# HGRN part of a hybrid decoder step: gate group ahead of the value group and between the levels; first half of the decay differences ahead of the fourth masked sum; last values product at the end of the tile

## The chip, the cores and the metric

The kernel runs on one core of one Trainium2 chip. The metric is the device time of one execution in microseconds (us), the median of several runs. Engines by the names of the profile: PE is TensorE, DVE VectorE, ACT ScalarE, POOL GpSimd, SP SyncE (which only issues transfers here).

## What is computed

One step of a one-layer hybrid decoder on 2048 prompt tokens and 64 sample tokens, model width 1024. The input projection has eight groups of 512 columns: four for an attention part, four for an HGRN2 part (query, forget, value, gate). The change concerns the HGRN2 part, a gated linear recurrence with 4 heads of 128 x 128 state:

```
b    = cumsum(log f)                                # over the tokens of a chunk
att  = q . k * exp(b_t - b_s)  for s <= t           # per channel, then summed
o    = att @ v + (q * exp(b)) @ S
S'   = exp(b_last) * S + (k * exp(b_last - b))^T @ v
out  = rms_norm(o) * silu(gate)                     # then the output projection
```

## The kernel before

The program has four passes, each closed by a barrier of all engines: `pass_projections` (projections of the attention groups for 17 tiles of 128 tokens, then the HGRN2 part), `pass_attention`, `pass_samples`, `pass_output`. Only the HGRN2 part of `pass_projections` is touched; it is written for each engine by hand, and the engines meet through semaphores. Each engine takes its instructions in the order written.

The HGRN2 part works on one tile t of 128 tokens per `step(t, ...)`, t = 0 to 15; in the same step PE projects the four groups of the next tile i = t + 1 and DVE, ACT and POOL prepare that tile's operands. A product of two fp32 values is made as three products of split operands (lines 92 to 94), 24 matmuls of 512 columns for a group, 6 for a quarter (`product_quarter`).

- `group(i, p, g)` (PE): group g = 0 query, 1 forget, 2 value, 3 gate. Before the change groups 0 and 2 land in PSUM bank 0, groups 1 and 3 in bank 1. A group waits until ACT has copied out what stood in its bank.
- `levels(t, h)` (PE, lines 876 and 877): for head h the seven masked parts of the decay products, 14 matmul rows in the trace, into two banks that all heads share; so levels of head h wait until DVE has multiplied those of head h - 1 by the mask.
- `keep_pairs(t, h)` (DVE): the mask product (line 737) and the masked sum (line 741), which gives `att`.
- `out_rows(t, pt, h)` (PE, lines 885 and 886): the values product `att @ v` plus the state's part; it waits for `att`.
- `key_rows`, `head_columns`, `gains` (PE): transposes of keys, of query and forget columns, and the state's gain.
- `forget(i)` (DVE, lines 747 to 752), `decays(i)` (ACT, logarithm, line 585), `cumulate(i)` (DVE, running sum, line 759): the decay of the next tile.
- `differences` (DVE): for each half of two heads 16 subtractions and copies in `decay_differences` (lines 127 to 136), into the buffer `lv[hf]`; the second half, hf = 1, waits until `out_rows` of head 3 has read that buffer.
- `exps(i, hf)` (ACT, line 589): the exponential of a half in place.
- `operands(i)` (POOL, `decay_products`, lines 145 to 150): for each half 14 products with q and k, in place.
- `gate_input`, `inputs_q`, `inputs_f`, `value_input`, `q_columns` (ACT): copies of projections out of PSUM with their activation. A change of function costs an ACT_TABLE_LOAD.
- `o_stats` (ACT), `o_norm`, `carry` (DVE), `gated` (POOL), `store` (SP): norm of the output rows, the new state, the gating and the store.
- `again(t)` (SP): loads the split x of tile t into one of two buffers when tile t - 2 has been projected.

Before the change the order of a step on PE is: group 0; levels 0; first half of group 1; levels 1; values 0; second half of group 1; levels 2; keys; values 1; head columns; levels 3; values 2; first half of group 2; values 3; second half of group 2; first half of group 3; gains; second half of group 3. On DVE: masked sums 0, 1, 2; forget; masked sum 3; cumulate; both halves of the differences; norm; carry. On ACT: gate of tile t; query and forget of tile i; keys; query columns; logarithm; exponential 0; values; exponential 1; norm.

Of the kernel before, what the change touches and what calls it, by code (L numbers as in the profile page):

```python
# [8 lines left out]
ACT = mybir.ActivationFunctionType  # L9
# [7 lines left out]
P = 128  # L17
# [4 lines left out]
NP = SEQ // P  # L22
NT = NP + 1
# [44 lines left out]
PIECES = 4  # L68
# [3 lines left out]
def after(eng, sem, count):  # L72

    if not isinstance(count, int) or count > 0:
        eng.wait_ge(sem, count)
# [44 lines left out]
def decay_differences(dve, b, lv, blocks, last, n0=0):  # L120

    for slot, width in blocks:
        b_lo, b_up, ref = level_views(b, width)
        d_lo, d_up, _ = level_views(lv[:, slot - n0, :], width)
        dve.tensor_tensor(d_up, b_up, ref, ALU.subtract)
        dve.tensor_tensor(d_lo, ref, b_lo, ALU.subtract)
    pair = b.rearrange("p (n w) -> p n w", w=2)
    first = pair[:, :, 0:1].broadcast_to([P, pair.shape[1], 2])  # L130
    dve.tensor_tensor(lv[:, LEAF_Q - n0, :].rearrange("p (n w) -> p n w", w=2), pair, first, ALU.subtract)
    dve.tensor_tensor(lv[:, LEAF_K - n0, :].rearrange("p (n w) -> p n w", w=2), first, pair, ALU.subtract)
    dve.tensor_copy(lv[:, LEAF_QE - n0, :], b)
    run = b.rearrange("p (n w) -> p n w", w=last)
    end = run[:, :, last - 1:last].broadcast_to([P, run.shape[1], last])
    return dve.tensor_tensor(lv[:, LEAF_KD - n0, :].rearrange("p (n w) -> p n w", w=last), end, run, ALU.subtract)  # L136
# [14 lines left out]
                              k[:, None, :].broadcast_to([P, 2, n]), ALU.mult)  # L151


LAST = NT - 1

EVICT = list(range(NP - 1)) + [LAST, NP - 1]
# [2 lines left out]
def pass_projections(nc, io, keep):  # L159


    with ExitStack() as ctx:
# [7 lines left out]
        w_hi = [sb(f"w_hi{g}", [P, KD, GW], F32R) for g in range(4)]  # L170
# [62 lines left out]
        def half(ap, hf):  # L233
            return ap[:, hf * 2 * P:(hf + 1) * 2 * P]

        def col(t):
            return rstd[:, t:t + 1]

        @block.sync
        def _(sp):  # L240
# [21 lines left out]
            def again(t):  # L262

                if t == 0:
                    sp.wait_ge(s["proj"][3], NT - 1)
                elif t == 1:
                    sp.wait_ge(s["proj"][3], NT)
                else:
                    sp.wait_ge(s["proj"][7], t - 1)
                sp.wait_ge(s["x2_store"][t % 2], 32 * (t // 2 + 1))  # L270
                sp.dma_start(f32(x_hi[t % 2][:, :, :]).rearrange("p k t -> p (k t)"), io["xh_s"][t]).then_inc(s["x2_load"][t % 2], 16)
                sp.dma_start(f32(x_lo[t % 2][:, :, :]).rearrange("p k t -> p (k t)"), io["xl_s"][t]).then_inc(s["x2_load"][t % 2], 16)
# [181 lines left out]
        def _(act):  # L454
# [7 lines left out]
            def pieces(g):  # L462
                for n in range(g * PIECES, (g + 1) * PIECES):
                    piece(n)
# [94 lines left out]
            def gate_input(i, p):  # L559
                act.wait_ge(s["proj"][7], i + 1)  # L560
                after(act, s["o_out"], i - 1)
                act.activation(gate[:, p], bank[1], ACT.Silu, scale=col(i)).then_inc(s["gate"], 1)

            def inputs_q(i):
                act.wait_ge(s["proj"][4], i + 1)
                after(act, s["qT_ps"], i)
                act.activation(q_tok, bank[0], ACT.Silu, scale=col(i)).then_inc(s["q_tok"], 1)

            def inputs_f(i):
                act.wait_ge(s["proj"][5], i + 1)  # L570
                after(act, s["sT_ps"], i)
                act.activation(s_tok, bank[1], ACT.Sigmoid, scale=col(i)).then_inc(s["s_tok"], 1)

            def q_columns(i):
                act.wait_ge(s["qT_ps"], i + 1)
                after(act, s["operands"], 2 * i)
                act.activation(qT, tps.rearrange("p h t -> p (h t)"), ACT.Copy).then_inc(s["qT"], 1)

            def value_input(i, p):
                act.wait_ge(s["proj"][6], i + 1)  # L580
                act.activation(v_tok[:, p], bank[0], ACT.Copy, scale=col(i)).then_inc(s["v_tok"], 1)

            def decays(i):
                act.wait_ge(s["f_clamped"], i + 1)
                act.activation(lfT, lfT, ACT.Ln).then_inc(s["log_f"], 1)

            def exps(i, hf):
                act.wait_ge(s["diff"], 2 * i + hf + 1)
                act.activation(lv[hf], lv[hf], ACT.Exp).then_inc(s["decay"], 1)  # L589
# [10 lines left out]

            def step(t, pt, more):
                i, p = t + 1, 1 - pt
                gate_input(t, pt)
                inputs_q(i)
                inputs_f(i)
                act.wait_ge(s["kdT_ps"], t + 1)
                after(act, s["gain_ps"], t)
                act.activation(kd_tok, kps.rearrange("p h d -> p (h d)"), ACT.Copy).then_inc(s["kd_tok"], 1)
                q_columns(i)
                decays(i)  # L610
                if more:
                    exps(i, 0)
                value_input(i, p)
                if more:
                    exps(i, 1)
                    tile_decay(p)
                o_stats(t)

            act.wait_ge(s["x_lo"], NT)
            inputs_q(0)  # L620
            pieces(7)
            inputs_f(0)
            act.wait_ge(s["store_q"][0], 32 * 9)
            act.wait_ge(s["store_q"][1], 32 * 8)
            q_columns(0)
            decays(0)
            exps(0, 0)
            value_input(0, 0)
            exps(0, 1)
            tile_decay(0)  # L630
            act.wait_ge(s["store_v"], 16 * NT)
            act.wait_ge(s["store_g"], 16 * NT)
            for t in range(NP):
                step(t, t % 2, t < NP - 1)
            gate_input(NP, 0)

        @block.vector
        def _(dve):
# [6 lines left out]
            def pieces(g):  # L645
                for n in range(g * PIECES, (g + 1) * PIECES):
                    piece(n)
# [79 lines left out]
            norm_qk(NP - 1)  # L727
            pieces(5)
            pieces(6)
            pieces(7)  # L730

            def keep_pairs(t, h):

# [26 lines left out]
                last.then_inc(s["cumsum"], 1)  # L760
                dve.wait_ge(s["cumsum"], i + 1)

            def differences(i, t):
                for hf in range(2):
                    if t is not None:
                        dve.wait_ge(s["av"], 4 * t + 2 * hf + 2)
                        dve.wait_ge(s["kdT_ps"], t + 1)
                    decay_differences(dve, half(bT, hf), lv[hf], all_levels, P).then_inc(s["diff"], 1)

            def o_norm(t):  # L770
                o3 = o_out.rearrange("p (h v) -> p h v", h=H)
# [16 lines left out]
            for p in range(2):  # L788
                dve.wait_ge(s["store_q"][p], 32 * (9 - p))
            forget(0)  # L790
            cumulate(0)
            differences(0, None)

            def step(t, pt, more):
                i = t + 1
                keep_pairs(t, 0)
                keep_pairs(t, 1)
                keep_pairs(t, 2)
                forget(i)
                keep_pairs(t, 3)  # L800
                if more:
                    cumulate(i)
                    differences(i, t)
                o_norm(t)
                carry(t, pt)

# [5 lines left out]
        def _(pe):  # L812
# [26 lines left out]
                job(g, LAST)  # L839
                job(g, NP - 1)  # L840

            def group(i, p, g, halves=(0, 1)):

                if 0 in halves:
                    pe.wait_ge(s["x2_load"][p], 32 * (i // 2 + 1))
                    if i == 0 and g < 2:
                        pe.wait_ge(s["qk_norm"], 2 * NT - 2)
                    after(pe, s[("v_tok", "gate", "q_tok", "s_tok")[g]], i if g < 2 else i + 1)
                for b in range(PIECES):
                    if b // 2 in halves:  # L850
                        if i == 0:
                            pe.wait_ge(s["w_lo"], (4 + g) * PIECES + b + 1)
                        mm = product_quarter(pe, bank[g % 2], x_hi[p], x_lo[p], w_hi[g], w_lo[g], b)
                if 1 in halves:
                    mm.then_inc(s["proj"][4 + g], 1)

            def head_columns(i, t):
# [46 lines left out]
            def step(t, pt):  # L904
                i, p = t + 1, 1 - pt
                group(i, p, 0)
                levels(t, 0)
                group(i, p, 1, (0,))
                levels(t, 1)
                out_rows(t, pt, 0)  # L910
                group(i, p, 1, (1,))
                levels(t, 2)
                key_rows(t)
                out_rows(t, pt, 1)
                head_columns(i, t)
                levels(t, 3)
                out_rows(t, pt, 2)
                group(i, p, 2, (0,))
                out_rows(t, pt, 3)
                group(i, p, 2, (1,))  # L920
                group(i, p, 3, (0,))
                gains(t, pt)
                group(i, p, 3, (1,))

            group(0, 0, 0)
            group(0, 0, 1)
# [1048 lines left out]
```

## Time and profile before

| | |
|---|---|
| median of 3 runs | 1761.52 us (1758.78 to 1763.17) |
| the profiled execution | 1758.49 us, of which its span 1756.7 us |
| mean granted TensorE clock | 0.962 |
| busy share of the span | PE 90%, DVE 56%, ACT 43%, POOL 28% |
| the HGRN2 steps | about 441 to 992 us of the span |

All times in the rows below are counted from the start of the span. Busy shares are averages over four passes with different limits; the steps are read from windows inside them.

### The profile page before, as it was taken

Reading aid. Unit: us, or ns where it says so; the run is one execution under the profiler, and the core shown is the slowest. Engines: PE = TensorE matmul, PEld = TensorE weight load, DVE = VectorE, ACT = ScalarE, POOL = GpSimd, SP = SyncE. Lnnn points to the kernel's source line nnn. Section 1 sums busy time; section 2 is a strip of 40 time slices with the busy share of each in tenths; the row PEclk is TensorE's granted clock in tenths of the full one; section 3 lists DMA queues with packets and bytes.
Section 4 is the critical chain, followed back from the end, with each engine's and each line's share of the span. In section 5 each row is a group of like instructions: output and inputs, shape, how many; then the busy total and the mean of one; then the engine's idle time right before and its main releaser. Section 6 shows DMA issues by size and latency. Waiting matters only on the chain. (4 is left out here: it accounts for less than half of the span.)

```text
span 1756.7 us, 25192 instructions
## 1 busy us (share of the span) xinstructions
PE 1577.5 (90%) x9156; PEld 1277.6 (73%) x9156; DVE 982.8 (56%) x2316; ACT 753.1 (43%) x1074; POOL 485.7 (28%) x636
## 2 busy tenths in 40 slices
PE   6799999997999999999999689999999568299998
PEld 5688888886887788778887567767777445177776
DVE  4322222254677667766776489888888624523332
ACT  5333333345444544453445266666666422211110
POOL 1433223341544664466446200000000010121211
PEclk9999999998999999999999889999999869699999
DMA  8444433445010101010100331000000286534442
GB/s 298 179 144 144 144 144 144 179 141 170 26 37 31 55 31 37 30 55 31 37 31 31 116 121 66 30 25 13 14 24 13 82 279 222 162 117 138 150 142 72
DMA packets 79762, 171.48 MB, mean 98 GB/s; under 512 B 9122, under 2 KB 15906, under 8 KB 79650
## 3 DMA queue, kind: packets, MB, share of 16 engines
q1 hardware_dynamic: 79650, 170.00, 28.0%
q8 instruction: 69, 1.13, 0.3%
q14 instruction: 43, 0.35, 0.1%
HBM read 113.35 MB, written 56.62 MB: 97 GB/s over the span
## 5 line engine op out<-in xcount | busy, mean ns | idle before, releaser
L92 PE MATMUL h_banks<-h_w_hi,h_x_hi 128*128 128x512 f32 x1088 | 435.4, 400 | 23.0 <-DVE h_x_lo L651 16.5
L94 PE MATMUL h_banks<-h_w_hi,h_x_lo 128*128 128x512 f32 x1088 | 426.9, 392 | 0.0
L93 PE MATMUL h_banks<-h_w_lo,h_x_hi 128*128 128x512 f32 x1088 | 426.7, 392 | 0.0
L92 PEld LDWEIGHTS h_banks<-h_w_hi,h_x_hi 128*128 128x128 f32 x1088 | 206.6, 190 | 65.9 <-DVE h_x_lo L651 17.3
L94 PEld LDWEIGHTS h_banks<-h_w_hi,h_x_lo 128*128 128x128 f32 x1088 | 206.0, 189 | 44.3
L93 PEld LDWEIGHTS h_banks<-h_w_lo,h_x_hi 128*128 128x128 f32 x1088 | 206.5, 190 | 40.7
L145 POOL TENSOR_TENSOR h_stage_or_levels<-h_stage_or_levels,h_qk_or_hgrn 128x128 f32<-128x128 f32 x192 | 105.8, 551 | 283.2 <-ACT h_stage_or_levels L589 283.2
L1078 ACT ACTIVATE p_scores<-p_scores,p_nmx 128x256 f32<-128x256 f32 (+15 forms) x128 | 153.1, 1196 | 5.6 <-DVE p_nmx L1129 5.4
L1214 PE MATMUL p_ops<-p_V,p_WT 128*128 128x128 f32 x1088 | 146.4, 280 | 8.8 <-ACT p_WT L1087 8.4
L1214 PEld LDWEIGHTS p_ops<-p_V,p_WT 128*128 128x128 f32 x1088 | 132.6, 193 | 15.6 <-ACT p_WT L1087 14.2
L1124 DVE CUSTOM_DVE_ANT_0 p_scores<-p_sps,p_zero 128x512 f32<-128x512 f32 x192 | 122.2, 686 | 15.8 <-PE p_sps L1188 15.6
L737 DVE TENSOR_TENSOR h_qk_or_hgrn<-h_banks,h_mask 128x896 f32<-128x896 f32 x64 | 69.7, 1090 | 105.7 <-PE h_banks L877 105.7
L1087 ACT ACTIVATE p_WT<-p_tps 128x512 f32<-128x512 f32 (+3 forms) x160 | 84.6, 529 | 84.7 <-PE p_tps L1201 84.4
L589 ACT ACTIVATE h_stage_or_levels<-h_stage_or_levels 128x2560 f32<-128x2560 f32 x32 | 75.1, 2347 | 102.6 <-DVE h_stage_or_levels L136 102.6
L83 PE MATMUL y_yps<-w_out_hi,y_mT_hi 128*128 128x512 f32 x272 | 111.0, 408 | 7.8 <-DVE y_yt L1850 6.4
L741 DVE TENSOR_REDUCE h_qk_or_hgrn<-h_qk_or_hgrn 128x128 f32<-128x896 f32 x64 | 111.2, 1738 | 2.2
L876 PE MATMUL h_banks<-h_stage_or_levels 128*128 128x128 f32 x768 | 97.7, 277 | 14.6 <-POOL h_stage_or_levels L150 14.6
L876 PEld LDWEIGHTS h_banks<-h_stage_or_levels 128*128 128x128 f32 x768 | 93.1, 191 | 23.9 <-POOL h_stage_or_levels L150 21.4
L1403 POOL MEMSET s_Q<- 128x1024 f32 x1 | 1.0, 951 | 393.6 <-POOLq L58 393.6
L83 PE MATMUL y_yps<-w_out_lo,y_mT_hi 128*128 128x512 f32 x272 | 108.5, 399 | 0.0
L83 PE MATMUL y_yps<-w_out_hi,y_mT_lo 128*128 128x512 f32 x272 | 108.4, 399 | 0.0
L402 POOL TENSOR_TENSOR h_qk_or_hgrn<-h_qk_or_hgrn,h_qkg 128x1024 f32<-128x1024 f32 x17 | 42.7, 2513 | 202.4 <-DVE h_qk_or_hgrn L673 202.4
(218 smaller groups left out, 2642.4 us busy)
## 6 DMA issues: line engine op xcount, KB each, us to landing
h_stage_or_levels<-in_w_in SPq DMA_DIRECT2D x32, 512.0 KB, 6.3
h_xs_sq_or_tok<-in_xT SPq DMA_DIRECT2D x17, 512.0 KB, 5.9
h_qk_or_hgrn<-in_x SPq DMA_DIRECT2D x17, 512.0 KB, 6.1
tmp_xh_s<-h_x_hi SPq DMA_DIRECT2D x17, 512.0 KB, 3.2
tmp_xl_s<-h_x_lo SPq DMA_DIRECT2D x17, 512.0 KB, 4.4
h_x_hi<-tmp_xh_s SPq DMA_DIRECT2D x17, 512.0 KB, 3.6
h_x_lo<-tmp_xl_s SPq DMA_DIRECT2D x17, 512.0 KB, 4.5
s_kc<-in_cache_k SPq DMA_DIRECT2D x32, 256.0 KB, 3.7
```

Of the source, the lines that this page charges most:

```text
L83: mm = eng.matmul(out, a[:, k, :], b[:, k, cols], start=(k == 0 and a is x_hi and b is w_hi), stop=(k == KD - 1 and a is x_lo))
L92: eng.matmul(out, x_hi[:, k, :], w_hi[:, k, :], start=(k == 0), stop=False)
L93: eng.matmul(out, x_hi[:, k, :], w_lo[:, k, :], start=False, stop=False)
L94: mm = eng.matmul(out, x_lo[:, k, :], w_hi[:, k, :], start=False, stop=(k == KD - 1))
L145: pool.tensor_tensor(e_up, e_up, q_up, ALU.mult)
L589: act.activation(lv[hf], lv[hf], ACT.Exp).then_inc(s["decay"], 1)
L741: dve.tensor_reduce(att[:, h % 2], masked.rearrange("p l t -> p t l"), AX.X, ALU.add).then_inc(s["att"], 1)
L876: pe.matmul(lps[:, n, :], l[:, n, c], l[:, n, c], start=True, stop=True)
L1078: act.activation(row, row, ACT.Exp, bias=nmx[:, n % 2, m:m + 1], accum_out=ls[:, u % 2, m, h:h + 1]).then_inc(s["exp"], 1)
L1087: act.activation(WT[:, g % 2, 0:w // P, :], tps[g % 2][:, 0:w // P, :], ACT.Copy).then_inc(s["wT"], 1)
L1124: dve.tensor_tensor_reduce(sc[m][:, n % (4 - m), c0:c0 + w], sps[k % 4][:, 0:w], add, SCALE, -3e38, ALU.add, ALU.max, mx[:, n % 2, m, c:c ...
L1214: mm = pe.matmul(ops[u % 2][:, h, :], WT[:, g % 2, b, :], V[:, kb, h * DV:(h + 1) * DV], start=(kb == 0), stop=(kb == TILES[u]))
```

## The change

The projection of the gate moves ahead of that of the values, in quarters placed between the levels; group 1 is done whole, right behind group 0, ahead of levels 0. From tile 1 on the gate lands in bank 0 and the values in bank 1 (`bank_of`). Head columns come after values 0, three places earlier. Values 3 (`out_rows` of head 3) closes the step. On DVE `forget` stands ahead of masked sum 2, `cumulate` and the first half of the differences ahead of masked sum 3, the second half behind it. On ACT the gate of tile i is copied between the logarithm and exponential 0, no longer the gate of tile t at the start of the step. SP's `again` waits for both the value and the gate group. Ahead of the first step, ACT's copy of the forget group and DVE's `forget(0)` stand ahead of the last weight pieces, and the copies of values and gate ahead of the exponentials.

```diff
+def bank_of(i, g):
+    if i > 0 and g >= 2:
+        return 3 - g
+    return g % 2
...
+                    sp.wait_ge(s["proj"][6], t - 1)
                     sp.wait_ge(s["proj"][7], t - 1)
...
             def step(t, pt, more):                      # scalar
                 i, p = t + 1, 1 - pt
-                gate_input(t, pt)
                 inputs_q(i)
                 inputs_f(i)
+                q_columns(i)
                 act.wait_ge(s["kdT_ps"], t + 1)
                 after(act, s["gain_ps"], t)
                 act.activation(kd_tok, ...)
-                q_columns(i)
                 decays(i)
+                gate_input(i, p)
                 if more:
                     exps(i, 0)
                 value_input(i, p)
...
             inputs_q(0)
+            inputs_f(0)
             pieces(7)
-            inputs_f(0)
...
             decays(0)
+            value_input(0, 0)
             exps(0, 0)
-            value_input(0, 0)
+            act.wait_ge(s["store_v"], 16 * NT)
+            act.wait_ge(s["store_g"], 16 * NT)
+            gate_input(0, 0)
             exps(0, 1)
...
-            gate_input(NP, 0)
...
-            pieces(7)                                   # vector
...
             forget(0)
+            pieces(7)
             cumulate(0)
...
                 keep_pairs(t, 0)
                 keep_pairs(t, 1)
+                forget(i)
                 keep_pairs(t, 2)
-                forget(i)
+                if more:
+                    cumulate(i)
+                    differences(i, t, 0)
                 keep_pairs(t, 3)
                 if more:
-                    cumulate(i)
-                    differences(i, t)
+                    differences(i, t, 1)
                 o_norm(t)
                 carry(t, pt)
...
             def step(t, pt):                            # tensor
                 i, p = t + 1, 1 - pt
                 group(i, p, 0)
+                group(i, p, 1)
                 levels(t, 0)
-                group(i, p, 1, (0,))
+                group(i, p, 3, (0,))
                 levels(t, 1)
                 out_rows(t, pt, 0)
-                group(i, p, 1, (1,))
+                head_columns(i, t)
+                group(i, p, 3, (1,))
                 levels(t, 2)
                 key_rows(t)
                 out_rows(t, pt, 1)
-                head_columns(i, t)
+                group(i, p, 3, (2,))
                 levels(t, 3)
                 out_rows(t, pt, 2)
+                group(i, p, 3, (3,))
                 group(i, p, 2, (0,))
+                group(i, p, 2, (1,))
+                gains(t, pt)
+                group(i, p, 2, (2, 3))
                 out_rows(t, pt, 3)
-                group(i, p, 2, (1,))
-                group(i, p, 3, (0,))
-                gains(t, pt)
-                group(i, p, 3, (1,))
```

In the new text of PE's `group` the last argument counts quarters, before it counted halves. `group` waits for the copy that last emptied its bank: for group 0 from tile 2 on that is the gate, for group 1 the values.

## Rows read from the trace of the kernel before

**Rows 1.** Windows: length; PE, PEld, DVE, ACT, POOL busy; clock, DMA share, GB/s.

```profile
685.00:720.00 35.00, 32.79 (x189) 28.18 (x189) 24.48 (x57) 16.61 (x18) 18.95 (x32) 1.00 0.11 38
```

**Rows 2.** Waits, 480 to 965 us: who waited for whom, us, times, longest.

```profile
PEld h_banks L885 <- DVE h_qk_or_hgrn L741: 22.5, 14, 1.6
...
PEld h_banks L876 <- POOL h_stage_or_levels L150: 19.0, 14, 1.4
```

**Rows 3.** One line's instructions: the key transposes, four in each of 16 tiles.

```profile
L893 PE MATMUL h_banks<-ident,h_stage_or_levels x64: 272/273/273, 452.0 to 974.9; 128*128 128x128 f32 x64
```

**Rows 4.** Timeline of PE in one tile: start, length, instruction, [idle before <- releaser].

```profile
683.77 0.39 PE L94 MATMUL h_banks<-h_w_hi,h_x_lo 128*128 128x512 f32 x1
...
685.09 1.60 PE L876 MATMUL h_banks<-h_stage_or_levels 128*128 128x128 f32 x12 [0.93 <-POOL h_stage_or_levels L150]
...
686.67 0.47 PE L92 MATMUL h_banks<-h_w_hi,h_x_hi 128*128 128x512 f32 x1
...
689.29 0.39 PE L94 MATMUL h_banks<-h_w_hi,h_x_lo 128*128 128x512 f32 x1
689.52 1.50 PE L876 MATMUL h_banks<-h_stage_or_levels 128*128 128x128 f32 x12
...
702.17 0.39 PE L94 MATMUL h_banks<-h_w_hi,h_x_lo 128*128 128x512 f32 x1
703.75 0.49 PE L885 MATMUL h_banks<-h_xs_sq_or_tok,h_qk_or_hgrn 128*128 128x128 f32 x2 [1.19 <-DVE h_qk_or_hgrn L741]
```

**Rows 5.** Timeline of DVE in the same tile.

```profile
686.95 1.09 DVE L737 TENSOR_TENSOR h_qk_or_hgrn<-h_banks,h_mask 128x896 f32<-128x896 f32 x1 [2.88 <-PE h_banks L877]
688.08 1.78 DVE L741 TENSOR_REDUCE h_qk_or_hgrn<-h_qk_or_hgrn 128x128 f32<-128x896 f32 x1
...
698.82 1.36 DVE L747 TENSOR_SCALAR h_qk_or_hgrn<-h_banks,h_lbt 128x128 f32<-128x128 f32 x4
...
705.00 0.29 DVE L127 TENSOR_TENSOR h_stage_or_levels<-h_qk_or_hgrn 128x128 f32<-128x128 f32 x1
...
708.31 0.42 DVE L136 TENSOR_TENSOR h_stage_or_levels<-h_qk_or_hgrn 128x256 f32<-128x256 f32 x1
...
711.07 0.42 DVE L131 TENSOR_TENSOR h_stage_or_levels<-h_qk_or_hgrn 128x256 f32<-128x256 f32 x1
...
711.94 0.42 DVE L136 TENSOR_TENSOR h_stage_or_levels<-h_qk_or_hgrn 128x256 f32<-128x256 f32 x1
```

**Rows 6.** Timeline of ACT in the same tile.

```profile
712.39 2.35 ACT L589 ACTIVATE h_stage_or_levels<-h_stage_or_levels 128x2560 f32<-128x2560 f32 x1 [0.71 <-DVE h_stage_or_levels L136]
...
716.95 1.28 ACT L562 ACT_TABLE_LOAD   x1
718.24 0.69 ACT L562 ACTIVATE h_xs_sq_or_tok<-h_banks,rstd 128x512 f32<-128x512 f32 x1
```

**Rows 7.** Timeline of POOL in the same tile: products of one half, then the next.

```profile
711.18 1.50 POOL L145 TENSOR_TENSOR h_stage_or_levels<-h_stage_or_levels,h_qk_or_hgrn 128x128 f32<-128x128 f32 x1 [15.98 <-ACT h_stage_or_levels L589]
712.64 0.46 POOL L146 TENSOR_TENSOR h_stage_or_levels<-h_stage_or_levels,h_qk_or_hgrn 128x128 f32<-128x128 f32 x1
...
719.84 0.45 POOL L145 TENSOR_TENSOR h_stage_or_levels<-h_stage_or_levels,h_qk_or_hgrn 128x128 f32<-128x128 f32 x1
```

**Rows 8.** Timelines of DVE and POOL before the steps, where both work on SBUF.

```profile
47.76 10.21 DVE L643 TENSOR_TENSOR h_w_lo<-h_stage_or_levels,h_w_hi 128x1024 fp32r<-128x1024 f32 x4
...
388.18 1.76 DVE L643 TENSOR_TENSOR h_w_lo<-h_stage_or_levels,h_w_hi 128x1024 fp32r<-128x1024 f32 x1
...
388.82 1.44 POOL L410 TENSOR_TENSOR h_qk_or_hgrn<-h_qk_or_hgrn 128x128 f32<-128x128 f32 x1
```

**Rows 9.** Timelines of PE, DVE and ACT ahead of the first step.

```profile
420.76 1.12 PE L867 MATMUL h_banks<-ident,h_xs_sq_or_tok 128*128 128x128 f32 x4 [9.43 <-ACT h_xs_sq_or_tok L572]
...
417.42 2.54 DVE L643 TENSOR_TENSOR h_w_lo<-h_stage_or_levels,h_w_hi 128x1024 fp32r<-128x1024 f32 x2 [0.26 <-ACT h_w_hi L460]
...
424.21 0.63 ACT L585 ACTIVATE h_qk_or_hgrn<-h_qk_or_hgrn 128x512 f32<-128x512 f32 x1 [1.72 <-DVE h_qk_or_hgrn L752]
```

More of the change, by code:

```diff
@@ L561, in gate_input @@
                 after(act, s["o_out"], i - 1)
-                act.activation(gate[:, p], bank[1], ACT.Silu, scale=col(i)).then_inc(s["gate"], 1)
+                act.activation(gate[:, p], bank[bank_of(i, 3)], ACT.Silu, scale=col(i)).then_inc(s["gate"], 1)
             def inputs_q(i):
@@ L580, in value_input @@
                 act.wait_ge(s["proj"][6], i + 1)
-                act.activation(v_tok[:, p], bank[0], ACT.Copy, scale=col(i)).then_inc(s["v_tok"], 1)
+                act.activation(v_tok[:, p], bank[bank_of(i, 2)], ACT.Copy, scale=col(i)).then_inc(s["v_tok"], 1)
             def decays(i):
@@ L626, in _ @@
             decays(0)
+            value_input(0, 0)
             exps(0, 0)
-            value_input(0, 0)
+            act.wait_ge(s["store_v"], 16 * NT)
+            act.wait_ge(s["store_g"], 16 * NT)
+            gate_input(0, 0)
             exps(0, 1)
             tile_decay(0)
-            act.wait_ge(s["store_v"], 16 * NT)
-            act.wait_ge(s["store_g"], 16 * NT)
             for t in range(NP):
                 step(t, t % 2, t < NP - 1)
-            gate_input(NP, 0)
         @block.vector
@@ L761, in cumulate, with differences @@
                 dve.wait_ge(s["cumsum"], i + 1)
[L763 to L768, printed above, removed]
+            def differences(i, t, hf):
+                if t is not None:
+                    dve.wait_ge(s["av"], 4 * t + 2 * hf + 2)
+                    dve.wait_ge(s["kdT_ps"], t + 1)
+                decay_differences(dve, half(bT, hf), lv[hf], all_levels, P).then_inc(s["diff"], 1)
             def o_norm(t):
@@ L790, in _ @@
             forget(0)
+            pieces(7)
             cumulate(0)
-            differences(0, None)
+            differences(0, None, 0)
+            differences(0, None, 1)
             def step(t, pt, more):
@@ L840, in _, with group @@
                 job(g, NP - 1)
-            def group(i, p, g, halves=(0, 1)):
-                if 0 in halves:
+            def group(i, p, g, parts=range(PIECES)):
+                k = bank_of(i, g)
+                if 0 in parts:
                     pe.wait_ge(s["x2_load"][p], 32 * (i // 2 + 1))
@@ L847, in group @@
                         pe.wait_ge(s["qk_norm"], 2 * NT - 2)
[L848 to L854, printed above, removed]
+                    elif g < 2:
+                        before = 2 if bank_of(i - 1, 2) == k else 3
+                        pe.wait_ge(s["v_tok" if before == 2 else "gate"], i)
+                    else:
+                        pe.wait_ge(s[("q_tok", "s_tok")[k]], i + 1)
+                for b in parts:
+                    if i == 0:
+                        pe.wait_ge(s["w_lo"], (4 + g) * PIECES + b + 1)
+                    mm = product_quarter(pe, bank[k], x_hi[p], x_lo[p], w_hi[g], w_lo[g], b)
+                if PIECES - 1 in parts:
                     mm.then_inc(s["proj"][4 + g], 1)
```

## The prediction, made before the changed kernel was run

> **What bounds the kernel now.** I read the windows first, then the waits, then one tile engine by engine. In the HGRN2 steps TensorE is busy 32.79 of 35 us at full granted clock, VectorE 24.48, GpSimd 18.95, ScalarE 16.61 [rows 1]: TensorE is the bound and only its idle time can be won. The list of waits gives two that end at TensorE once in each of 14 tiles: its weight loads wait 1.6 us for the masked sum of head 3 ahead of values 3, and 1.4 us for GpSimd's products ahead of levels 0 [rows 2]. The tile repeats every (974.9 - 0.3 - 452.0) / 15 = 34.84 us, 0.3 standing for the last tile's other three transposes, of 272 ns that overlap [rows 3].
>
> In the timeline a matmul of 512 columns follows its forerunner after 0.23 us, and levels 1 come 0.23 us behind the last matmul ahead of them [rows 4]. So levels 0 could start at 684.00 and do so at 685.09, and values 3 could start at 702.40 and do so at 703.75 [rows 4]. That is 1.09 + 1.35 = 2.44 us lost per tile; without it a tile takes 32.40.
>
> **The change part by part, time 0 being the start of levels 0.**
>
> *Levels 0.* Both projections of 5.5 us now stand ahead of them, and the products they wait for come earlier (below). The 1.09 us go if GpSimd is done by then.
>
> *The quarters.* Levels 1 need the first mask product, done at 686.95 + 1.09 - 685.09 = 2.95 [rows 5]. Before, a half group (2.85 us) covered that; now it is a quarter: levels 0 take 1.58, six matmuls 6 x 0.23 = 1.4 and the entry into a group 0.1 (a half group takes 2.85 where 12 x 0.23 is 2.76) [rows 4], so levels 1 could start at 3.05. The cover is nearly gone: I count 0.1. Values 0 need the masked sum, which ends at 688.08 + 1.78 - 685.09 = 4.77 [rows 5]; they would be due at about 4.6: 0.15. One more entry into a group: 0.1. Together 0.35 per tile, between 0.1 and 1.0 (each of the two waits off by 0.3).
>
> *Values 3.* A masked sum with its mask product takes 2.9 us [rows 5]. VectorE ends sum 0 at 4.8 and sum 1 at 7.8. Forget, one masked sum and cumulate take 705.00 - 698.82 = 6.18 before [rows 5], and the same three follow now: 14.0. The first half of the differences takes 708.31 + 0.42 - 705.00 = 3.73 [rows 5]: 17.7; sum 3 ends at 20.6. Values 3 are due one tile less two groups and themselves later: 32.75 - 11.1 - 0.4 = 21.25. So the 1.35 us go, with 0.6 to spare.
>
> *Gate copy.* Between logarithm and exponential 0 it brings a second table load: 1.28 + 0.69 + 1.28 = 3.25 us of ScalarE [rows 6]. The gate is projected by about 15.0, so it ends with both loads at about 17.0, hidden behind the differences that end at 17.7. Without that cover the delay would meet GpSimd's slack below. Exponential 0 ends at 20.1 (2.35 us) [rows 6].
>
> *Second half of the differences.* It now waits for values 3: 21.25 + 0.6 = 21.9, so it no longer follows the first half directly. Behind it on VectorE stand norm and carry; behind its exponential on ScalarE stand norm statistics and the next query copy, for which the gate's first quarter in the next tile waits. From the end of exponential 1 to the end of the first copy behind the table load takes 718.24 + 0.69 - 714.74 = 4.2 [rows 6]. Undisturbed: differences end at 25.6, exponential 28.0, query copy 32.2; it is due at 32.75 + 1.58 = 34.3. Slack 2.1.
>
> *The meeting that the old order did not have.* GpSimd's products of the first half now run from 20.2, and take 719.84 - 712.64 + 0.4 = 7.6 us [rows 7]; the second half of the differences starts at 21.9, in the middle. Both read two SBUF operands. What the trace shows of this: GpSimd's first product took 1.50 where the next, as large, took 0.46; it started at 711.18, inside the differences, and ended with them, having waited through four VectorE instructions (the first from 711.07, the last ending at 712.36) [rows 5, 7]. On the other hand VectorE waits too: four subtractions of 1.27 each took 10.21 us beside GpSimd's work, and GpSimd's product of 128 x 128 took 1.44 while VectorE went between it and the one before [rows 8, 9]. Those subtractions each wait for a semaphore and signal one (line 643); the differences wait once and then run 16 in a row. I take what the nearest row shows, the same differences against the same products: VectorE gets in after at most one product (0.4) and keeps GpSimd out until it is done. Then the first products end at 20.2 + 7.6 + 3.7 = 31.5, ahead of levels 0 at 32.75; the second end at 39.1, ahead of levels 2 at about 40.3. Cost 0. The other end is GpSimd first: at 21.9 it has done 1.7 of its 7.6 us, and VectorE comes 5.9 late, 5.9 - 2.1 = 3.8 beyond the slack.
>
> The Trainium skill (page SBUF — State Buffer, section Who interferes with whom) says that a VectorE instruction with two SBUF inputs contends with a GpSimd instruction that reads SBUF, and that whichever issues first holds the pair for the whole instruction. Rows 8 agree. Rows 5 and 7 do not fit a lock that changes hands after every instruction, for GpSimd lost three handovers; by a strict turn-taking the sum would be that of the first rival below.
>
> *Loads and stores.* `again` waits for one semaphore more. The values group ends the tile, where the gate group did, so the load moves by less than a group and still has most of a tile. Behind it on SP stands a store needed a tile later: 0.
>
> *Ahead of step 0.* TensorE waits 9.43 us for the forget copy, which stood behind the weight pieces [rows 9]. That is not the gain: the logarithm decides, which ended at 424.84. The weight pieces end on VectorE at 419.96, so on ScalarE about 1.25 earlier, 418.7 [rows 9]; query columns (0.6), a table load (1.28) and the logarithm (0.63) then end at 421.2. Gain 3.6, once. The gate copy now stands between the exponentials (3.25), hidden by the 7.6 us of the first products; uncovered it would cost 3.25 once.
>
> *End of the last tile.* Values 3 come last, but the last gate copy behind the last group is gone: 0, between -1 and +3, the 4.2 us chain less what followed the last group before.
>
> **Sum.** A tile 32.40 + 0.35 = 32.75, 2.1 less; 15 x 2.1 = 31.4, plus 3.6 = 35. The profiled execution took 1758.5, the median 1761.5, 3.0 more. 1758.5 - 35 + 3.0 = 1726. Its own range: 0.1 to 1.0 in place of 0.35 is -4 to +10, the tail up to +3: 1718 to 1738.
>
> **Rivals.** *First, GpSimd wins the meeting.* The second half of the differences takes turns with the products or waits until they are through. For it: rows 8, and 9 or 10 of 14 products are still open at 21.9. Against it: the 1.50 us of rows 7, alike in every tile. Price: query copy 3.3 to 3.8 late (each gate's first quarter waits that much, with values 3 moving along), a tile of 36.0 to 36.5: +1.2 to +1.7, 18 to 25 over 15 tiles, less 3.6: 1776 to 1783. It decides from a delay of 2.1 (slack) + 2.1 (gain) + 0.2 (the start, spread) = 4.4 us of that half; below 2.1 it costs nothing.
>
> *Second, the tight places give back part.* Levels 1, values 0, values 3 (0.6 spare) and exponential 0 (0.7 spare) have no cover worth the name. If each loses 0.3, a tile takes 33.9: -14 - 3.6: 1744, say 1738 to 1756.
>
> *Third, the wait only moves.* The meeting splits so that the half comes about 4 us late: a tile of 34.8, and the start's 3.6 alone remains: 1756 to 1766. It needs a finely shared port, which neither set of rows shows.
>
> **Chances.** Forecast 0.60, first rival 0.19, second 0.16, third 0.05. A change of 0.3% (5.3 us) is what a measurement can tell: faster 0.76, same 0.05, slower 0.19. The range for 8 in 10 takes in forecast, second and third: 1717 to 1766; the slower case, 0.19, lies outside.
>
> **What would show it.** Right: no wait of values 3 for line 741 of over 0.3 us, none of levels 0 for line 150; key transposes 32.7 apart; the second half's 16 instructions in 3.7 to 4.1 us while one GpSimd product lasts about 4; the query copy (line 567) never awaited. Wrong: differences of 0.3 us stretched to 0.6 and more or their first held for 5 us, and a new wait of TensorE for line 567 ahead of the gate's first quarter.

## The result, and the profile after

The changed kernel took 1767.81 us (median of 12 runs, 1762.49 to 1773.21), the kernel before 1760.80 in the same comparison (12 runs, 1756.29 to 1764.67). The ratio is 1.0041 with an interval of 1.0026 to 1.0056: slower by 0.4%, where 1726 us was forecast. The profiled execution has a span of 1766.1 us, 9.4 more than before, and busy shares of PE 90%, DVE 60% (56% before), ACT 44%, POOL 27%.

Both waits that the change was predicted to remove are gone [rows 2]. One new wait has come. The waits between 470 and 965 us of the changed kernel (engine, line, whom it waited for: us in total, times, longest; the fifteenth tile's wait lies behind the window):

```profile
ACT h_stage_or_levels L597 <- DVE h_stage_or_levels L136: 123.6, 28, 8.0
...
PE h_banks L92 <- ACT h_xs_sq_or_tok L575: 34.9, 14, 2.5
```

In each of 14 tiles TensorE waits 2.5 us for the copy of the query (line 575), and ScalarE's exponential up to 8.0 us for the last difference (line 136). One tile shows why. First VectorE, the timeline of the changed kernel (start, length, instruction, [idle before]):

```profile
702.52 0.29 DVE L127 TENSOR_TENSOR h_stage_or_levels<-h_qk_or_hgrn 128x128 f32<-128x128 f32 x1
...
705.83 0.42 DVE L136 TENSOR_TENSOR h_stage_or_levels<-h_qk_or_hgrn 128x256 f32<-128x256 f32 x1
...
710.21 0.35 DVE L127 TENSOR_TENSOR h_stage_or_levels<-h_qk_or_hgrn 128x128 f32<-128x128 f32 x1 [1.12 <-PE h_banks L899]
710.49 0.55 DVE L128 TENSOR_TENSOR h_stage_or_levels<-h_qk_or_hgrn 128x128 f32<-128x128 f32 x1
...
714.34 1.37 DVE L128 TENSOR_TENSOR h_stage_or_levels<-h_qk_or_hgrn 128x128 f32<-128x128 f32 x1
715.63 1.38 DVE L127 TENSOR_TENSOR h_stage_or_levels<-h_qk_or_hgrn 128x128 f32<-128x128 f32 x1
716.93 0.28 DVE L128 TENSOR_TENSOR h_stage_or_levels<-h_qk_or_hgrn 128x128 f32<-128x128 f32 x1
...
718.01 0.41 DVE L136 TENSOR_TENSOR h_stage_or_levels<-h_qk_or_hgrn 128x256 f32<-128x256 f32 x1
```

The first half of the differences takes 705.83 + 0.42 - 702.52 = 3.73 us, as before [rows 5]. The second half, 16 instructions of the same shapes, takes 718.01 + 0.41 - 710.21 = 8.21. Now GpSimd in the same stretch:

```profile
708.70 0.46 POOL L145 TENSOR_TENSOR h_stage_or_levels<-h_stage_or_levels,h_qk_or_hgrn 128x128 f32<-128x128 f32 x1 [12.50 <-ACT h_stage_or_levels L597]
...
710.37 0.51 POOL L145 TENSOR_TENSOR h_stage_or_levels<-h_stage_or_levels,h_qk_or_hgrn 128x128 f32<-128x128 f32 x1
710.85 0.51 POOL L146 TENSOR_TENSOR h_stage_or_levels<-h_stage_or_levels,h_qk_or_hgrn 128x128 f32<-128x128 f32 x1
...
714.23 1.34 POOL L148 TENSOR_TENSOR h_stage_or_levels<-h_stage_or_levels,h_qk_or_hgrn 128x512 f32<-128x512 f32 x1
715.52 1.33 POOL L150 TENSOR_TENSOR h_stage_or_levels<-h_stage_or_levels,h_qk_or_hgrn 128x512 f32<-128x512 f32 x1
```

GpSimd was in its fourth product when VectorE came. From then on the two go one by one: the differences from 710.49 to 713.82 start 0.46 to 0.53 apart, which is one small product each, two take 1.37 and 1.38 beside the products of 1.34 and 1.33 us, and once GpSimd is through (716.85) a difference takes 0.28 again. GpSimd hardly loses: 14 products take 716.85 - 708.70 = 8.15 us against 7.6 before. What the 4.48 us of delay do, on ScalarE:

```profile
718.45 2.35 ACT L597 ACTIVATE h_stage_or_levels<-h_stage_or_levels 128x2560 f32<-128x2560 f32 x1 [7.99 <-DVE h_stage_or_levels L136]
...
724.30 0.69 ACT L575 ACTIVATE h_xs_sq_or_tok<-h_banks,rstd 128x512 f32<-128x512 f32 x1
```

The exponential of the second half starts at 718.45, and the query copy, with two table loads between, ends at 724.99. TensorE's timeline:

```profile
720.91 1.50 PE L889 MATMUL h_banks<-h_stage_or_levels 128*128 128x128 f32 x12
...
725.13 0.47 PE L92 MATMUL h_banks<-h_w_hi,h_x_hi 128*128 128x512 f32 x1 [2.50 <-ACT h_xs_sq_or_tok L575]
...
726.60 2.73 PE L889 MATMUL h_banks<-h_stage_or_levels 128*128 128x128 f32 x12
...
732.48 1.50 PE L889 MATMUL h_banks<-h_stage_or_levels 128*128 128x128 f32 x12
```

Levels 0 no longer wait; the gate's first quarter waits 2.50 us for the copy. Levels 1 behind it take 2.73 us, levels 2 only 1.50 for the same 12 matmuls. The windows say why (length; PE, PEld, DVE, ACT, POOL busy; clock, DMA share, GB/s):

```profile
723.00:726.00 3.00, 0.87 (x4) 0.76 (x5) 2.91 (x8) 2.96 (x3) 3.00 (x8) 1.00 0.00 0
...
727.00:728.00 1.00, 1.00 (x6) 1.00 (x6) 0.73 (x1) 0.00 (x0) 1.00 (x2) 0.50 0.06 16
...
729.00:730.00 1.00, 1.00 (x7) 1.00 (x7) 0.21 (x1) 0.00 (x0) 0.92 (x2) 0.50 0.00 0
...
732.00:757.00 25.00, 25.00 (x138) 21.61 (x137) 21.45 (x47) 10.88 (x9) 8.11 (x14) 1.00 0.16 53
```

Behind the idle 2.50 us the granted clock falls to 0.50, the level of 1.2 GHz, for some 3 us. It does so in 6 of the 14 tiles and costs 1.65 us there: by the starts of levels 0, eight tiles take 34.83 to 34.89 us and six 36.47 to 36.53, in a mixed order. The first tile, which has no late half ahead of it, takes 472.00 - 439.39 = 32.61.

The balance against the span of before, +9.4 us: 15 tiles, by the first and the last levels 0, (969.85 - 439.39) - (963.79 - 441.21) = +7.9; the start -1.8; from the last levels 0 to the attention's first matmul 40.65 instead of 39.05, +1.6; the rest, +1.7, lies behind it, where the change has nothing.

### The profile page after: what moved, and what is told of

Same layout as the page of the kernel before. It is cut to its first block and busy times, and to the rows that moved or that the text cites. A ratio compares the mean times of both kernels' runs of the same rounds, so it can differ in the third digit from the quotient of the medians.

```text
span 1766.1 us, 25209 instructions
## 1 busy us (share of the span) xinstructions
PE 1580.8 (90%) x9156; PEld 1288.8 (73%) x9156; DVE 1052.3 (60%) x2316; ACT 776.9 (44%) x1091; POOL 476.2 (27%) x636
## 5 line engine op out<-in xcount | busy, mean ns | idle before, releaser
L145 POOL TENSOR_TENSOR h_stage_or_levels<-h_stage_or_levels,h_qk_or_hgrn 128x128 f32<-128x128 f32 x192 | 93.6, 487 | 295.3 <-ACT h_stage_or_levels L597 295.3
L1229 PEld LDWEIGHTS p_ops<-p_V,p_WT 128*128 128x128 f32 x1088 | 132.9, 193 | 15.6 <-ACT p_WT L1102 14.0
L889 PEld LDWEIGHTS h_banks<-h_stage_or_levels 128*128 128x128 f32 x768 | 102.7, 204 | 7.3 <-POOL h_stage_or_levels L150 1.5
L889 PE MATMUL h_banks<-h_stage_or_levels 128*128 128x128 f32 x768 | 103.5, 288 | 0.9 <-POOL h_stage_or_levels L150 0.9
L669 DVE TENSOR_REDUCE h_ss<-h_xs_sq_or_tok 128x8 f32<-128x512 f32 x34 | 21.8, 680 | 133.4 <-ACT h_xs_sq_or_tok L494 133.4
L127 DVE TENSOR_TENSOR h_stage_or_levels<-h_qk_or_hgrn 128x128 f32<-128x128 f32 x192 | 88.2, 459 | 18.0 <-PE h_banks L899 17.4
```

The costliest lines, as they stand in the source:

```text
L145: pool.tensor_tensor(e_up, e_up, q_up, ALU.mult)
L889: pe.matmul(lps[:, n, :], l[:, n, c], l[:, n, c], start=True, stop=True)
L1229: mm = pe.matmul(ops[u % 2][:, h, :], WT[:, g % 2, b, :], V[:, kb, h * DV:(h + 1) * DV], start=(kb == 0), stop=(kb == TILES[u]))
```

## The experiments

Theory: the only loss is the meeting of the second half with GpSimd's products, one VectorE instruction per product, and what TensorE's clock makes of the wait. Rivals: the tight places or the later values cost the time; the delay comes from the order of the sums; the long tiles have another cause. Tile lengths are (start of the last levels 0 - start of the first) / 15; the runs of the kernel before in the same comparisons had medians of 1762.06 (stop after 4, sum 3 first, values 3 early, meeting put into before) and 1761.38 us (the other three).

| kernel | 16 differences of the second half, us | TensorE's wait for the query copy, us | tile, us | median, us | ratio to before |
|---|---|---|---|---|---|
| before | 3.7 | none | 34.84 | | |
| changed | 8.21 | 2.5 | 35.36 | 1767.81 | 1.0041 [1.0026, 1.0056] |
| stop after 4 products | 3.74 | none | 32.43 | 1725.44 | 0.9778 [0.9750, 0.9806] |
| stop after 10 products | 5.31 | none | 32.44 | 1719.95 | 0.9763 [0.9734, 0.9793] |
| stop after 13 products | 7.11 | 1.4 | 33.70 | 1741.09 | 0.9888 [0.9865, 0.9910] |
| filler matmuls | 8.20 | 0.65 | 34.82 | 1758.46 | 0.9984 [0.9966, 1.0002] |
| sum 3 first | 3.73, in one tile 6.38 | none, in that tile 0.67 | 33.68 | 1739.79 | 0.9875 [0.9850, 0.9901] |
| values 3 early | 3.7 | none | 32.85 | 1728.31 | 0.9802 [0.9779, 0.9824] |
| meeting put into before | 8.77 | 6.0, for the gate copy | 42.10 | 1879.80 | 1.0665 [1.0635, 1.0695] |

**GpSimd stops after its fourth product** of the first half until VectorE's second half is through.

```diff
 def decay_products(..., pause=None):
     for slot, width in blocks:
+        if pause is not None and slot == pause[0]:
+            pool.wait_ge(pause[1], pause[2])
...
+    pause=(2, s["diff"], 2 * i + 2) if hf == 0 else None
```

> The changed kernel, with GpSimd waiting behind the fourth of the 14 products of the first half until VectorE has finished the second half of the differences. Theory (the two meet at a shared SBUF port and take turns, so that half comes 4.5 us late, and the query copy, TensorE's new wait of 2.5 us and the clock dips follow): the 16 differences take 3.7 us again, TensorE no longer waits for the query copy, no tile of 36.5, every tile about 32.6 (the first tile of the changed kernel, which has no wait, took 32.61); 7 x 1.65 + 15 x 2.25 = 45 us less, about 1722. Rival (the wait comes from values 3 standing at the end of the tile, so that norm and query copy come late whatever GpSimd does): the wait stays at 2 us or more, 1760 or above.

The timeline of GpSimd in this run, and VectorE's entry:

```profile
728.29 0.46 POOL L148 TENSOR_TENSOR h_stage_or_levels<-h_stage_or_levels,h_qk_or_hgrn 128x128 f32<-128x128 f32 x1
732.41 0.46 POOL L147 TENSOR_TENSOR h_stage_or_levels<-h_stage_or_levels,h_qk_or_hgrn 128x128 f32<-128x128 f32 x1 [3.66 <-DVE h_stage_or_levels L136]
```

```profile
728.59 0.31 DVE L127 TENSOR_TENSOR h_stage_or_levels<-h_qk_or_hgrn 128x128 f32<-128x128 f32 x1 [1.15 <-PE h_banks L902]
728.82 0.28 DVE L128 TENSOR_TENSOR h_stage_or_levels<-h_qk_or_hgrn 128x128 f32<-128x128 f32 x1
```

The 16 differences take 3.74 us, the list of TensorE's waits between 470 and 965 us is empty, the tiles from the second on are 32.41 to 32.43 us apart, and in the windows from 700 to 780 us TensorE is busy throughout at a clock of 1.00. Nothing else of the change was touched, so the whole loss is the meeting with what it sets off, and the tight places cost nothing. The median is 3 us above the expected time. In the profiled execution (1728.32 us) the steps began at 447.35 instead of 439.39 us; it was late already at the first head columns (421.01 against 412.49), ahead of all that the edit touches.

**GpSimd stops later.** The same wait, placed before the eleventh product, and before the last of 14.

> A smaller dose. GpSimd stops before its eleventh product of the first half. VectorE comes in at the fourth, so some 7 differences wait for a product each (0.47 us in place of 0.20): 3.73 + 7 x 0.27 = 5.6 us for the 16. That is 1.9 us late, and the slack of the query copy, read from the changed kernel, is 4.48 - 2.5 = 2.0: no wait or one of a few tenths, a tile of 32.4 to 32.7, 1725 to 1730 us. Rival (there is no slack, each delay of the half goes into the tile): 15 x 1.9 = 28 us over the run that stops after four products, 1754.

> Dose of the meeting. As the changed kernel, but GpSimd stops before its last product of the first half (13 of 14 done) until VectorE's second half of the differences is through. Turn-taking (one VectorE instruction per GpSimd product): of the 8.21 us that the 16 differences took in the changed kernel, one turn beside a large product goes (1.37 becomes 0.28): 7.1 us. TensorE's wait for the query copy falls from 2.5 to 1.4 us, a tile is 33.8 us where the clock holds. 15 tiles x (35.4 - 33.8) = 24 us less than the changed kernel: 1744 us; if the granted clock still falls behind the shorter wait in half of the tiles, 1.65 us each, 1756. Rival (the meeting is all or nothing, any meeting delays the half until GpSimd is through): differences as long as before, 1768.

VectorE around the point where GpSimd stops after 10 products:

```profile
688.29 0.29 DVE L127 TENSOR_TENSOR h_stage_or_levels<-h_qk_or_hgrn 128x128 f32<-128x128 f32 x1 [1.24 <-PE h_banks L902]
688.50 0.55 DVE L128 TENSOR_TENSOR h_stage_or_levels<-h_qk_or_hgrn 128x128 f32<-128x128 f32 x1
...
690.84 0.55 DVE L127 TENSOR_TENSOR h_stage_or_levels<-h_qk_or_hgrn 128x128 f32<-128x128 f32 x1
691.30 0.28 DVE L128 TENSOR_TENSOR h_stage_or_levels<-h_qk_or_hgrn 128x128 f32<-128x128 f32 x1
...
693.19 0.41 DVE L136 TENSOR_TENSOR h_stage_or_levels<-h_qk_or_hgrn 128x256 f32<-128x256 f32 x1
```

and where it stops after 13, with TensorE's waits from 470 to 965 us:

```profile
699.68 1.37 DVE L128 TENSOR_TENSOR h_stage_or_levels<-h_qk_or_hgrn 128x128 f32<-128x128 f32 x1
700.98 0.28 DVE L127 TENSOR_TENSOR h_stage_or_levels<-h_qk_or_hgrn 128x128 f32<-128x128 f32 x1
...
702.26 0.41 DVE L136 TENSOR_TENSOR h_stage_or_levels<-h_qk_or_hgrn 128x256 f32<-128x256 f32 x1
```

```profile
PE h_banks L92 <- ACT h_xs_sq_or_tok L578: 21.0, 15, 1.4
```

The differences take 0.55 us beside GpSimd's small products, 1.37 beside the large one, and 0.28 from the instruction on at which it stops. After 10 products the half ends 1.6 us late (5.31 - 3.73) and no tile is longer; after 13 it ends 3.4 late and each waits 1.4; in the changed kernel 4.48 late and 2.5. So the slack of the query copy is 2.0 us, and behind it each microsecond of the half is one of the tile while the clock holds. The wait of 1.4 us brought no fall of the clock: the tiles are 33.76 to 33.82 us throughout, and the windows from 470 to 925 us show 1.00. The expected 1744 was the branch without it; 1741.09 is 3 us below. With the stop after 10 products the tile is as expected, but 1719.95 lies 5 us below the expected band: in its profiled execution the steps began at 439.41 us, 7.9 earlier than with the stop after 4.

**Matmuls that nobody needs, in the wait.** They isolate the clock; their results are overwritten.

```diff
                 levels(t, 0)
+                for _ in range(8):
+                    pe.matmul(kps..., x_hi[p][:, 0, :], w_hi[0][:, 0, :], start=True, stop=True)
                 group(i, p, 3, (0,))
```

> As the changed kernel, but TensorE multiplies 8 matrices of 512 columns that nobody needs (into the keys' bank, which is written anew before it is read) between levels 0 and the gate's first quarter, 8 x 0.23 = 1.9 us of the 2.5 in which it waits for the query copy. Theory: the 36.5 us tiles differ from the 34.85 us ones by the granted clock alone, which falls behind the idle 2.5 us. With 0.6 us idle it stays at 1.00 and all tiles take 34.85: 15 x 34.85 = 522.8 in place of 530.5, some 8 to 11 us less than the changed kernel, 1757 to 1760. The meeting stays: the 16 differences take 8.2 us. Rival (the clock falls for another cause, or the long tiles are long for another cause): 7 tiles stay at 36.5, 1768.

```profile
717.69 2.10 PE L923 MATMUL h_banks<-h_w_hi,h_x_hi 128*128 128x512 f32 x8
720.43 0.47 PE L92 MATMUL h_banks<-h_w_hi,h_x_hi 128*128 128x512 f32 x1 [0.65 <-ACT h_xs_sq_or_tok L575]
...
721.88 1.50 PE L889 MATMUL h_banks<-h_stage_or_levels 128*128 128x128 f32 x12
...
726.15 1.50 PE L889 MATMUL h_banks<-h_stage_or_levels 128*128 128x128 f32 x12
```

The wait is 0.65 us, the query copy is no earlier, levels 1 take 1.50 like levels 2, and from the second tile on every tile takes 34.86 to 34.88. The long tiles (six, not seven as the expectation has it) were long by the clock alone, and the clock fell behind the idle time, which the matmuls filled. Median against median, of two comparisons, that is 1767.81 - 1758.46 = 9.4 us; with it, the changed kernel would stand where the kernel before stands.

**Sum 3 ahead of the differences**, as before the change, the rest as changed: the two halves then stand closer together.

```diff
-                    differences(i, t, 0)
                 keep_pairs(t, 3)
                 if more:
+                    differences(i, t, 0)
                     differences(i, t, 1)
```

> The changed kernel, with masked sum 3 back ahead of the first half of the differences; values 3 stay at the end of the tile. Now VectorE is already inside the second half when the first half's exponential ends, so GpSimd is the one that arrives. Theory (who streams first keeps the other out or makes it wait at each instruction): 16 differences in 3.7 us, the first product stretched to 1.5 to 3 us, the products about 1 us too late for levels 0, a tile of 33.3 to 33.6, no clock dip, about 1733 to 1737. Rival (values 3 at the end is the price): TensorE's wait for the query copy stays, 1760 or above.

Here the meeting has the other order: VectorE is in its second half (697.72 to 701.44) when GpSimd comes.

```profile
699.01 2.75 POOL L145 TENSOR_TENSOR h_stage_or_levels<-h_stage_or_levels,h_qk_or_hgrn 128x128 f32<-128x128 f32 x1 [13.66 <-ACT h_stage_or_levels L597]
701.72 0.46 POOL L146 TENSOR_TENSOR h_stage_or_levels<-h_stage_or_levels,h_qk_or_hgrn 128x128 f32<-128x128 f32 x1
```

```profile
699.14 0.28 DVE L128 TENSOR_TENSOR h_stage_or_levels<-h_qk_or_hgrn 128x128 f32<-128x128 f32 x1
699.35 0.28 DVE L127 TENSOR_TENSOR h_stage_or_levels<-h_qk_or_hgrn 128x128 f32<-128x128 f32 x1
...
701.03 0.41 DVE L136 TENSOR_TENSOR h_stage_or_levels<-h_qk_or_hgrn 128x256 f32<-128x256 f32 x1
```

GpSimd's first product takes 2.75 us, the next, as large, 0.46, while VectorE keeps its 0.28 per instruction: GpSimd is kept out until the stream ends, while nine more differences start. So it goes in 14 of the 15 tiles (2.72 to 2.76 us). In the odd one, GpSimd also came into VectorE's second half, which had run since 462.02, and yet the two took turns, VectorE first, then GpSimd:

```profile
463.04 0.28 DVE L128 TENSOR_TENSOR h_stage_or_levels<-h_qk_or_hgrn 128x128 f32<-128x128 f32 x1
463.24 0.55 DVE L127 TENSOR_TENSOR h_stage_or_levels<-h_qk_or_hgrn 128x128 f32<-128x128 f32 x1
```

```profile
463.16 0.48 POOL L145 TENSOR_TENSOR h_stage_or_levels<-h_stage_or_levels,h_qk_or_hgrn 128x128 f32<-128x128 f32 x1 [15.52 <-ACT h_stage_or_levels L597]
463.60 0.52 POOL L146 TENSOR_TENSOR h_stage_or_levels<-h_stage_or_levels,h_qk_or_hgrn 128x128 f32<-128x128 f32 x1
```

There the half takes 6.38 us, and TensorE waits 0.67 us for the query copy. GpSimd began 0.12 us into the running difference, in the other 14 tiles 0.06 to 0.11; whether that decides is not shown.

Where GpSimd is kept out, its products are late, the levels' weight loads wait for them 15.6 us in 28 cases, and a tile takes 33.76 us where 33.3 to 33.6 was expected; 1739.79 is 3 us above the expected band. The expectation's rival, that values 3 at the end is the price, falls, for the wait for the query copy is gone in 14 tiles. That the order of the sums alone is the price cannot be settled here, where the order was put back; the stops settle it, which keep the changed order and lose the wait.

**Values 3 early**: sum 3 ahead of the running sum, both halves behind it, values 3 behind the values' first quarter.

```diff
                 keep_pairs(t, 2)
+                keep_pairs(t, 3)
                 if more:
                     cumulate(i)
                     differences(i, t, 0)
-                keep_pairs(t, 3)
-                if more:
                     differences(i, t, 1)
...
                 group(i, p, 2, (0,))
+                out_rows(t, pt, 3)
                 group(i, p, 2, (1,))
                 gains(t, pt)
                 group(i, p, 2, (2, 3))
-                out_rows(t, pt, 3)
```

> The changed kernel, with masked sum 3 ahead of cumulate and both halves of the differences together as before the change, and values 3 right behind the first quarter of group 2. Theory: both halves end before GpSimd has done more than its first product, which waits 1 to 1.5 us; products done at about 31.9 after levels 0, where 32.5 is the tile; no wait of TensorE over 0.2 us, a tile of 32.4 to 32.7, 1718 to 1724. The rival, that values 3 at the end is the price, expects the same here; if the gain of the new group order itself is only apparent (tight places), a tile of 33.5 or more and 1735 or above.

Again VectorE streams first and GpSimd's first product takes 1.49 us (1.50 before, [rows 7]). The tile is 32.85 us, above the expected 32.4 to 32.7 and 0.42 more than with the stop after 4 products. The weight loads of the levels wait 10.9 us for issue (for nothing that the profile shows) in 30 cases against 4.2 in 15 there, (10.9 - 4.2) / 14 = 0.48 per tile; that fits by size, but its cause is not shown. The time came out 4 us above the expectation, which had no such term.

**The meeting put into the kernel before**: its second half also waits for the value copy, so that it comes when GpSimd has begun.

```diff
 for hf in range(2):                 # differences of the kernel before
...
+    if hf == 1:
+        dve.wait_ge(s["v_tok"], i + 1)
```

> The kernel before, with one wait more: the second half of the differences also waits for the value copy of the same tile, which there ends at about 0.6 us after GpSimd has begun the first half's products. So the same meeting in the old order. Theory (turns at the port): the 16 differences take 7.5 to 8.5 us in place of 3.7, each of the first dozen 0.5 or more in place of 0.28; the half ends about 7 us later than before, TensorE waits 3 to 5 us more for the gate copy, tiles of 38 to 40, 1805 to 1840. Rival (no contention, the new order alone stretches them): 3.7 us, half 3 us later, a tile of at most 35.5, 1772 or less.

VectorE in one tile, and the windows behind TensorE's wait in another:

```profile
725.72 0.39 DVE L127 TENSOR_TENSOR h_stage_or_levels<-h_qk_or_hgrn 128x128 f32<-128x128 f32 x1 [3.08 <-ACT h_xs_sq_or_tok L581]
726.04 0.54 DVE L128 TENSOR_TENSOR h_stage_or_levels<-h_qk_or_hgrn 128x128 f32<-128x128 f32 x1
...
734.08 0.41 DVE L136 TENSOR_TENSOR h_stage_or_levels<-h_qk_or_hgrn 128x256 f32<-128x256 f32 x1
```

```profile
699.00:700.00 1.00, 0.94 (x2) 0.84 (x3) 0.96 (x2) 0.98 (x2) 1.00 (x3) 0.50 0.00 0
700.00:701.00 1.00, 1.00 (x4) 0.77 (x3) 1.00 (x1) 0.80 (x1) 1.00 (x1) 0.50 0.00 0
...
703.00:704.00 1.00, 1.00 (x8) 0.91 (x7) 0.00 (x0) 0.00 (x0) 0.92 (x2) 1.00 0.00 0
```

The half starts at 725.72, 3.1 us after VectorE was ready, and takes 8.77 instead of 3.73: the meeting costs 5.0 us of that half in a kernel that has nothing else of the change, and the added wait 3.1 more. The tile of 42.10 us and the time of 1879.80 are above the expected 38 to 40 and 1805 to 1840: TensorE's new wait is 6.0 us (89.7 us in 15 tiles), which leaves a slack of 2.1 out of the 8.1 us of delay, and behind it the clock stands at 0.50. There, matmuls of 512 columns start 0.42 to 0.43 us apart instead of 0.23, and at 703 the clock is back at 1.00. The expectation had no term for the clock.

## Why the prediction was wrong

- **Levels 0 and values 3: right.** Both waits are gone [rows 2], in the changed kernel and in all runs that kept its order.
- **The quarters: right, and on the safe side.** The text gave 0.35 us per tile for tight places and a tile of 32.75. The first tile of the changed kernel took 32.61, and without the meeting 32.41: the second rival, at 0.16, has nothing for it.
- **Gate copy and its table load: right.** They are hidden; no wait of TensorE names them.
- **The slack of the query copy: right.** Forecast 2.1. The changed kernel (4.48 late, a wait of 2.5), the stop after 13 products (3.4 and 1.4) and the one tile of sum 3 first (6.38 - 3.72 = 2.66 and 0.67) all give 2.0; with the stop after 10, 1.6 late, nothing waits.
- **The meeting: the step that failed.** "VectorE gets in after at most one product (0.4) and keeps GpSimd out until it is done ... Cost 0." VectorE did get in after one product, but at every instruction anew, and GpSimd was not kept out. The half came 4.48 us late, 2.5 beyond the slack. The step was taken from the nearest row, 1.50 us [rows 7], in which the order of arrival was the opposite one: there VectorE had been streaming and GpSimd came second (its product ended at 712.68, 0.3 us behind the last difference, not with it). The run with sum 3 first shows that this row was read rightly for that order in 14 of 15 tiles (some 2.75 us kept out); it says nothing of the other order. The subtractions of 10.21 us [rows 8], which the text set aside because they wait and signal one by one, were the better guide: they take turns. There VectorE had begun first (47.76, GpSimd at 48.35), as in the odd tile of sum 3 first, so the order of arrival alone does not decide; what else does is open.
- **The rivals.** The other end of that cost was 5.9 us late, up to 3.8 beyond the slack; the measured 4.48 lies between. By mechanism the first rival (0.19) was nearest: the half takes turns with the products, and TensorE waits for the query copy. Its price was too high, and strict turn-taking is not the sum that the prediction put it equal to, for eleven differences ran between the products instead of behind them. By size the third rival was nearest, "the half comes about 4 us late", a tile of 34.8, and got 0.05; eight tiles took 34.83 to 34.89. That the other six come out at the first rival's 36.0 to 36.5 is chance: they are long by the 1.65 us of half clock behind the wait, a term that stands in no sum of the prediction. That term, about 9 us by the filler run, carries the result from the third rival's range beyond the upper end of 1766. Without it the prediction's break-even, a delay of 4.4 us, holds: in the filler run the half is some 4.5 us late, and the time is that of before (0.9984 [0.9966, 1.0002]).
- **The start**: 1.8 us instead of 3.6. The first levels 0 start at 439.39; the weight pieces were staged 2.1 us later than before in this execution (415.59 against 413.52), so the logarithm came forward less. In the profiled executions of the changed kernel and its six variants the first levels 0 start at 437.15 to 447.35, so one execution does not measure this term.
- **The tail**: 0 was taken, -1 to +3 allowed; +1.6 with the wait in the last tile. With the stop after 10 products it is 964.02 - 925.95 = 38.07 us, 1.0 less than before.

The Trainium skill (page SBUF — State Buffer, section Who interferes with whom) says that whichever engine issues first gets the shared port pair for the whole instruction. For VectorE coming second the trace agrees: each difference waits for one product. For GpSimd coming second the rule is mostly too short: in 14 of 15 tiles with sum 3 first it was held while nine more VectorE instructions started (2.75 us), and only in one did it get in within one instruction. The prediction weighed that rule and gave it too little, for it read the one order as if it were both.

Without the meeting the change is worth what the forecast said, and a little more: the stop after 10 products took 1719.95 us (1716.23 to 1725.03), 2.4% less than before, where 1726 had been forecast. It is one wait of GpSimd more than the changed kernel, and faster than both kernels. The two stops, after 4 and after 10 products, are not told apart: their intervals overlap and their tiles are equal.

## What to carry to other kernels

When a reorder makes VectorE's operations with two SBUF inputs and GpSimd's run at the same time, ask which of them is already streaming, and read a row with that order of arrival. Without such a row take turn-taking, one GpSimd instruction for each VectorE instruction, as the price; it came up in one tile even where VectorE had streamed first. If the late one has slack behind it, let the other stop for it by a semaphore; here the products could wait 3.7 us at no cost. And price a new wait of TensorE not by its length alone: look at the granted clock of the windows behind it.

## What was not expected of the hardware

- Sharing is not symmetric, with one exception. Where the differences were streaming and GpSimd's products came second, GpSimd was held until the stream ended in 53 of 54 meetings of all the runs (1.49 to 1.50 us, or some 2.75 us) and took turns in one. Where VectorE's differences came second and the products went on, they got one instruction between any two products in all 75 (in the changed kernel 16 differences in 8.21 us instead of 3.73, while 14 products take 8.15 instead of 7.6). Why the two engines differ, and what let GpSimd in that once, is not shown.
- Behind TensorE's idle 2.5 us the granted clock fell to the 1.2 GHz level for some 3 us in 6 of 14 tiles and not in the other eight, whose waits were alike (all 2.44 to 2.52); what chooses between them is open. Behind waits of 0.65 and 1.4 us no tile of these runs was longer by it.
- The profiled executions differ by up to 10 us in when the first step begins (437.15 to 447.35 us for the changed kernel and its variants, which are the same on TensorE up to there), ahead of which only projections and loads stand. In the two late ones ScalarE waited 42 us for loads of x between 340 and 440 us, in the changed kernel 14.7. Tile lengths behind the first repeat to 0.02 us with a stop after 4 or 10 products and to 0.15 us with sum 3 first, while the interval of a ratio is 5 to 11 us wide: for an effect inside the loop the tile is the better measure.
